# The last pair of row tiles of a feed-forward stage taken token third by token third, and a wait of its own for each table of the rotation

## The reference

```python
def _layer_norm(x, g, b):
    xc = xf - jnp.mean(xf, -1, keepdims=True)
    var = jnp.mean(xc * xc, -1, keepdims=True)
    return xc * lax.rsqrt(var + LN_EPS) * g + b

def _post_block(x, mix, w1, w3, w2, g1, b1, g2, b2):
    x = _layer_norm(ALPHA * x + mix, g1, b1)
    ff = (jax.nn.silu(x @ w1) * (x @ w3)) @ w2
    return _layer_norm(ALPHA * x + ff, g2, b2)
```

## Time and profile before

| | |
|---|---|
| median of 3 runs | 3449.32 us (3448.13 to 3454.1) |
| the profiled execution's own time | 3458.74 us |
| its span | 3457.0 us, 48614 instructions |
| mean granted TensorE clock | 0.913 of full speed |
| PE busy | 3005.5 us, 87%, 19603 matmuls |
| DVE, ACT, POOL busy | 1620.0 us (47%), 835.4 us (24%), 245.8 us (7%) |
| matmul of 128 x 352, float32 (L163 to L165) | 322 to 329 ns each, overlapping |
| add from PSUM to `k.xT` (L848), 24 a pair | 521 ns each |
| cast of a pair of weight tiles, 128 x 2048 (L155) | 1220 ns each |
| TensorE clock in 40 slices of the span, tenths | 9999899986899999999997995558999999999998 |
| PE busy in the same slices, tenths | 8998799969899999999995978007889999999995 |

### The profile page before, as it was taken

The page is one execution under the profiler, slowest core; times in us unless marked ns, Lnnn a source line. Parts: engine busy times, 40 slices in busy tenths (PEclk is TensorE's granted clock), DMA queues, the critical chain, the costliest instruction groups (busy, mean ns, idle before and its releaser), DMA issues. The chain is left out here.

```text
span 3457.0 us, 48614 instructions
## 1 busy us (share of the span) xinstructions
PE 3005.5 (87%) x19603; PEld 2730.4 (79%) x19603; DVE 1620.0 (47%) x3000; ACT 835.4 (24%) x1555; POOL 245.8 (7%) x279
## 2 busy tenths in 40 slices
PE   8998799969899999999995978007889999999995
PEld 8998466538799999999995956004589999999995
DVE  2111288747464443334445134996356333443336
ACT  2110166632432000000013112645433000000002
POOL 2000100005000000000001820002200000000000
PEclk9999899986799999999997995558999999999998
DMA  6222310040211011111101430001020111011101
GB/s 232 98 86 106 116 50 2 1 150 33 89 37 62 37 47 40 57 42 38 40 11 59 127 120 1 1 0 50 1 74 37 49 62 38 37 49 38 62 13 50
DMA packets 63287, 193.63 MB, mean 56 GB/s; under 512 B 7812, under 2 KB 32292, under 8 KB 53792
## 3 DMA queue, kind: packets, MB, share of 16 engines
q1 hardware_dynamic: 58176, 172.86, 14.2%
q0 software_dynamic: 3904, 12.46, 1.2%
q10 hardware_dynamic: 1008, 5.41, 0.4%
HBM read 159.68 MB, written 35.36 MB: 56 GB/s over the span
## 5 line engine op out<-in xcount | busy, mean ns | idle before, releaser
L163 PE MATMUL f_up<-f_x_high,f_w_first 128*128 128x352 f32 x1056 | 347.8, 329 | 21.8 <-issue 21.8
L165 PE MATMUL f_up<-f_x_high,f_w_first 128*128 128x352 f32 x1056 | 345.2, 327 | 0.0
L163 PE MATMUL f_up<-f_x_high,f_w_second 128*128 128x352 f32 x1056 | 344.6, 326 | 0.0
L164 PE MATMUL f_up<-f_x_low,f_w_first 128*128 128x352 f32 x1056 | 342.8, 325 | 0.0
L165 PE MATMUL f_up<-f_x_high,f_w_second 128*128 128x352 f32 x1056 | 342.6, 324 | 0.0
L164 PE MATMUL f_up<-f_x_low,f_w_second 128*128 128x352 f32 x1056 | 340.3, 322 | 0.0
L834 DVE TENSOR_TENSOR f_gated<-f_silu,f_up 128x352 f32<-128x352 f32 x120 | 62.5, 521 | 571.6 <-PE f_up L165 571.6
L163 PE MATMUL f_down<-f_h_high,f_w_high 128*128 128x352 f32 x960 | 314.3, 327 | 14.6 <-DVE xT_sb L871 5.7
L164 PE MATMUL f_down<-f_h_low,f_w_high 128*128 128x352 f32 x960 | 309.6, 323 | 0.0
L165 PE MATMUL f_down<-f_h_high,f_w_low 128*128 128x352 f32 x960 | 309.4, 322 | 0.0
L848 DVE TENSOR_TENSOR xT_sb<-xT_sb,f_down 128x352 f32<-128x352 f32 x384 | 198.6, 521 | 160.6 <-PE f_down L165 160.6
(11 more groups left out here) (467 smaller groups left out, 5891.5 us busy)
## 6 DMA issues: line engine op xcount, KB each, us to landing
f_raw<-w SPq DMA_DIRECT2D x66, 1024.0 KB, 4.8
pe<-pe_y SPq DMA_DIRECT2D x27, 528.0 KB, 2.9
pe_raw<-w_in_e SPq DMA_DIRECT2D x27, 512.0 KB, 4.0
po<-po_y SPq DMA_DIRECT2D x14, 528.0 KB, 2.9
po_raw<-w_in_o SPq DMA_DIRECT2D x14, 512.0 KB, 4.2
xT_sb<-xT ACTq DMA_DIRECT2D x4, 1056.0 KB, 11.5
ro_x<-po SPq DMA_DIRECT2D x8, 528.0 KB, 4.5
y<-xT_sb SPq DMA_DIRECT2D x3, 1408.0 KB, 5.2
```

Source lines behind the costliest of these rows:

```text
L163: pe.matmul(out, wh, xh, start=n == 0, stop=False)
L164: pe.matmul(out, wh, xl, start=False, stop=False)
L165: return pe.matmul(out, wl, xh, start=False, stop=n == depth - 1)
```

## The change

In `rope`, each table gets a semaphore of its own, and each engine waits only for the table that it reads. The order of the loads becomes rotm, first row tile, sin, cos. In the last pair of `project_and_feed`, PE now makes both tiles for one third, and then multiplies this third by w2 for all 8 output tiles, before it goes to the next third; silu and the hidden state follow in that order on ACT and DVE. The layer norm of a finished third goes among the up matmuls of the next, and its reciprocal and scaling among that third's adds. The w2 parts of the last pair go to `late_high` and `late_low`, which share the places of `raw13` and `raw2`. The squares of the second layer norm go to `oT`, and their sums to the place of `x_high` (`over_high`).

```diff
@@ rope
-        consts, scaled, swapped, turned, done, stored = map(st.sem, ("consts", "scaled", ...))
+        scaled, swapped, turned, done, stored = map(st.sem, ("scaled", ...))
+        rot_loaded, cos_loaded, sin_loaded = map(st.sem, ("rot_loaded", "cos_loaded", "sin_loaded"))
+                sp.dma_start(rotm[:], k.d["c_rot"]).then_inc(rot_loaded, 16)
                 load(0)
-                for dst, src in ((rotm, "c_rot"), (cos, "c_cos"), (sin, "c_sin")):
-                    sp.dma_start(dst[:], k.d[src]).then_inc(consts, 16)
+                sp.dma_start(sin[:], k.d["c_sin"]).then_inc(sin_loaded, 16)
+                sp.dma_start(cos[:], k.d["c_cos"]).then_inc(cos_loaded, 16)
...
-                pool.wait_ge(consts, 48)
+                pool.wait_ge(cos_loaded, 16)
...
-                pe.wait_ge(consts, 48)
+                pe.wait_ge(rot_loaded, 16)
...
-                dve.wait_ge(consts, 48)
+                dve.wait_ge(sin_loaded, 16)
@@ project_and_feed, buffers
+        with Stage(nc, name + "_aside0") as tmp:
+            over_high = tmp.sb("s", [P, KT, T])
         high = st.sb("x_high", [P, KT, T], F32R)
-        raw13 = st.sb("raw13", [P, 2, KT, P])
+        with Stage(nc, name + "_raw") as tmp:
+            raw13 = tmp.sb("13", [P, 2, KT, P])
+        late_high = st.sb("late_high", [P, 2, KT, P], F32R)
...
-        raw2 = st.sb("raw2", [P, 2, KT, P])
+        with Stage(nc, name + "_raw_") as tmp:
+            raw2 = tmp.sb("2", [P, 2, KT, P])
+        late_low = st.sb("late_low", [P, 2, KT, P], F32R)
...
+            bank = {0: 0, 1: 1, NCH: 1, NCH + 1: 0, NCH + 2: 1}
@@ project_and_feed, PE
-                make(2 * LAST, 0)
-                make(2 * LAST + 1, 1)
...
-                    return first13[:, 0, f - 2, m], first13[:, 1, f - 2, m]
+                    return late_high[:, f - 2, m], late_low[:, f - 2, m]
...
-                pe.wait_ge(w2_split, LAST + 1)
-                pe.wait_ge(h_split, PAIRS * 2 * NCH)
                 for c in range(NCH):
+                    for f in range(2):
+                        s = 2 * NCH * LAST + 2 * c + f
+                        if c == 0:
+                            pe.wait_ge(w13_split, 2 * LAST + f + 1)
+                        pe.wait_ge(h_split, s - NCH + 1)
+                        if c == 2 and f == 0:
+                            pe.wait_ge(root, NCH + 1)
+                        half(f, c, s % NCH, 0, gate)
+                        if c and f == 0:
+                            mean(NCH + c - 1)
+                        half(f, c, s % NCH, 1, value)
+                    if c:
+                        variance(NCH + c - 1)
+                    pe.wait_ge(w2_split, PAIRS)
+                    pe.wait_ge(h_split, 2 * NCH * LAST + 2 * c + 2)
                     for m in range(KT):
                         n = c * KT + m
                         pe.wait_ge(added, (LAST - 1) * outs + n - 1)
                         multiply(pe, down[:, n % 2, 0:CH], lambda f: weights(f, m), lambda f: hidden(f, c), 4).then_inc(product, 1)
-                        if c and m == 2:
-                            mean(NCH + c - 1)
-                    if c:
-                        variance(NCH + c - 1)
@@ project_and_feed, ACT
-                step(act, LAST, 0)
                 for c in range(NCH):
-                    square(NCH + c)
-                    deviation(NCH + c)
-                    affine(NCH + c)
+                    for f in range(2):
+                        s = 2 * NCH * LAST + 2 * c + f
+                        silu(s, s % NCH)
+                        if c and f == 0:
+                            square(NCH + c - 1)
+                        if c == 0 and f == 0:
+                            act.wait_ge(product, (LAST - 1) * outs)
+                        hidden_high(s, f, c)
+                    if c:
+                        deviation(NCH + c - 1)
+                        affine(NCH + c - 1)
+                square(2 * NCH - 1)
+                deviation(2 * NCH - 1)
+                affine(2 * NCH - 1)
@@ project_and_feed, DVE
-                steady(LAST, 0, 0)
-                dve.wait_ge(w2_loaded, PAIRS * 16)
-                dve.wait_ge(value, (2 * LAST + 1) * NCH)
-                split_on(dve, w2_high, PAIRS, w2_split, raw2[:], first13[:, 0], first13[:, 1])
-                steady(LAST, 0, 1)
...
+                for c in range(NCH):
                     j = NCH + c - 1
+                    for f in range(2):
+                        s = 2 * NCH * LAST + 2 * c + f
+                        if c and f == 0:
+                            centre(j)
+                        hidden(s, 0, f, c, s % NCH)
+                        if c and f == 0:
+                            sum_squares(j)
+                        if c == 0 and f == 0:
+                            dve.wait_ge(w2_loaded, PAIRS * 16)
+                            split_on(dve, w2_high, PAIRS, w2_split, raw2[:], late_high[:], late_low[:])
+                    if c:
+                        invert(j)
+                        add_last(c, [0, 1])
+                        scale(j)
+                        add_last(c, range(2, KT))
                     else:
+                        add_last(c, range(KT))
                     sum_up(j + 1)
-                invert(2 * NCH - 2)
-                scale(2 * NCH - 2)
                 centre(2 * NCH - 1)
                 sum_squares(2 * NCH - 1)
```

More of the change, by code:

```diff
@@ L346, in rope @@
         swap = st.ps("swap", [P, 2, NCH, 512])
-        consts, scaled, swapped, turned, done, stored = map(st.sem, ("consts", "scaled", "swapped", "turned", "done", "stored"))
+        scaled, swapped, turned, done, stored = map(st.sem, ("scaled", "swapped", "turned", "done", "stored"))
+        rot_loaded, cos_loaded, sin_loaded = map(st.sem, ("rot_loaded", "cos_loaded", "sin_loaded"))
         x_loaded = st.slots("x_loaded", RING)
@@ L446, in project_and_feed, with squares, square_sums @@
         spare = lambda j: aside[1 if j == NCH - 1 else 0]
-        squares = lambda j: spare(j)[:, 0:KT * CH].rearrange("p (n t) -> p n t", n=KT)
-        square_sums = lambda j: spare(j)[:, 3 * n_w:3 * n_w + CH]
+        def squares(j):
+            return spare(j)[:, 0:KT * CH].rearrange("p (n t) -> p n t", n=KT) if j < NCH else oT[:, :, cols(j - NCH)]
+        def square_sums(j):
+            return spare(j)[:, 3 * n_w:3 * n_w + CH] if j < NCH else over_high[:, 0, cols(j - NCH)]
         X_high = lambda n, c: high[:, n, cols(c)]
@@ L454, in stats @@
         def stats(j):
-            return (down[:, 0, 0:CH], down[:, 1, 0:CH]) if j == NCH - 1 else (up[:, 0, j % NCH, 0:CH], up[:, 1, j % NCH, 0:CH])
+            bank = {0: 0, 1: 1, NCH: 1, NCH + 1: 0, NCH + 2: 1}
+            return (down[:, 0, 0:CH], down[:, 1, 0:CH]) if j == NCH - 1 else (up[:, 0, bank[j], 0:CH], up[:, 1, bank[j], 0:CH])
         def middle(eng, step):
@@ L871, in add_last @@
                         dve.tensor_tensor(out=xm, in0=xm, in1=down[:, n % 2, 0:CH], op=ALU.add).then_inc(added, 1)
-                add_last(0, range(KT))
-                sum_up(NCH)
-                for c in range(1, NCH):
+                for c in range(NCH):
                     j = NCH + c - 1
[L877 to L882, removed]
-                    else:
[L884 to L888, removed]
+                    for f in range(2):
[13 more added lines that the diff above has]
+                        add_last(c, range(2, KT))
+                    else:
+                        add_last(c, range(KT))
                     sum_up(j + 1)
-                invert(2 * NCH - 2)
-                scale(2 * NCH - 2)
                 centre(2 * NCH - 1)
```

## The result

The changed kernel takes 3440.85 us (median of 19 runs, 3431.91 to 3457.61), the kernel before 3454.18 us beside it (19 runs, of which the 3449.32 above took the first three). The ratio is 0.9962, 95% interval [0.9953, 0.9971]: faster by 0.38%, 13.1 us (10.0 to 16.2). The forecast was 12.0 us.

What follows compares the result with a forecast made beforehand. PE, busy 87% of the span, was taken as the bound, leaving its idle time and work behind its last matmul. Stages 8.2 plus rotations 3.8 gave 12.0 us, from 3449.32 to 3437.3 us; range 3430 to 3446.

Steps and rivals of the forecast that it cites:

- The end of a stage: From the last down matmul's start to the last scaling: 22.1 us instead of 28.1, 6.0 us less per feed-forward stage.
- Bubbles: Last pair: PE waits for the hidden state three times, not once, +4.0 us; variance matmul inside the wait, −0.6.
- The first bubble's second condition: Last pair, first third: w2 must be split before the second hidden tile's gating; +0.3 us per stage.
- Stalls by DVE: Last pair: PE waits less for DVE's centring and scaling, 1.0 us against 2.8, so −1.8 us per stage.
- The clock: Last pair: PE's clock halves after the first bubble only, as before, costing 1.5 us; no fall in the other two.
- Rival 1: Last pairs: the clock falls in the two new bubbles as well, 6.0 us back, 3443.3 us; 13%.
- Table loads: Feed-forward stages: alternating silu and root tables add two loads per stage, 1.28 us each, root 0.02 behind, no drain.
- Rival 3: Each table switch idles a further 1.28 us ahead of the root, 5.1 us back, 3442.4 us; 5%.
- The rotations: Separate table waits: first add 2.85 us earlier, less 0.9 at the end; 1.9 us gained per rotation, 3.8 for two.
- Rival 2: The rotations gain nothing, because POOL and cos set their pace; 3441.1 us; 10%.
- rival 4: Last pairs: w2 lands 7.8 us after issue instead of 4.9, 5.8 us back over both stages, 3443.1 us; 5%.
- rival 5: Last pairs: the low clock outlasts the 12 matmuls after each bubble, kernel slower than before, 3460 us; 7%.

Runs made afterwards that it cites:

- e3: Changed kernel, but DVE makes the middle third's reciprocal and scaling after the last third's adds and sum, as before the change; ratio 0.9986 to the kernel before.
- e5: Changed kernel, but DVE waits for and splits w2 after the first third's second hidden tile instead of before it; ratio 0.9984 to the kernel before.
- e9: The changed kernel itself, run and profiled again; 3443.54 us, ratio 0.9956 to the kernel before.
- e6: Changed kernel, but the rotations load in the old order: first row, rotm, cos, sin; ratio 0.9951 to the kernel before.
- e7: Changed kernel, but the rotations load cos before sin: rotm, first row, cos, sin; ratio 0.9939 to the kernel before.
- e1: Kernel before with only the rotations changed (new `rope`, old `project_and_feed`); ratio 0.9986 to the kernel before, 4.8 us faster.
- e2: Kernel before with only the last pair of each feed-forward stage changed (old `rope`); ratio 0.9977 to the kernel before, 8.0 us faster.
- e4: Changed kernel, but each third first issues 12 down matmuls of the pair before last, then waits for the last pair's operands; ratio 0.9945 to the kernel before.
- e8: As e4, but in the second and third thirds DVE makes two adds before the reciprocal and two more before scaling; ratio 0.9925 to the kernel before.
- e10: The kernel of e8 with cos loaded before sin as in e7; 3430.82 us, ratio 0.9921 to the kernel before.

## Why the prediction was right, step by step

- **The end of a stage** (22.1 forecast instead of 28.1). It measured 22.2 and 22.2. e3 takes away alone what DVE's order gives of it. This step carries the gain of the feed-forward part; the other terms together cost a little. The sign given for it was misread from its own sum: 11.3 is where the squares end. They start at 8.8, by the sum and in the trace.
- **Bubbles** (+4.0, −0.6). Both new gaps are 2.15 from start to start, the variance inside them. Right.
- **The first bubble's second condition** (+0.3). It came to +0.06. The split ended 16.1 us after the pair's start, as I had it, but the gating could not have begun before 15.9 (0.43 behind the last up matmul's start), and it began at 16.0. That the cover is gone is right. e5 shows it, and so does the load's own scatter: where w2 landed after 4.77 us (f0 of e9) the gap was 2.14, where it landed after 5.06 (f0 of e6) it was 2.43.
- **Stalls by DVE** (−1.8, leaving 1.0). Too cautious: there remain 0.1 and 0.15 per third, 0.5 in the stage, −2.3. PE's span up to the last down matmul grew by 1.1 us in f1 (101.97 to 103.07), not 1.9; the two mis-sized terms make the difference.
- **The clock.** One fall per stage, behind the first gap, as before, was forecast. It came in f1, not in f0, and f0 is 1.7 shorter for it. Over all profiles with a first gap of 2.1 to 2.4 the fall came 14 times of 16. The two gaps without it were 2.16 and 2.17, and a gap of 2.14 had one, so their length doesn't tell them apart; what does is open. Behind the gaps with the variance inside it came in none of 28. Rival 1 is refuted.
- **Table loads.** The root starts 0.02 behind the load's end, also here. The drain that the Trainium skill ("ScalarE: Activation LUTs", section What ACT_TABLE_LOAD costs) adds is not in this trace. Rival 3 is refuted.
- **The rotations** (1.9 each). They gained 2.3 and 2.9 us, 1.4 more than forecast for the two. The step that was off is "cos is now the last table, so POOL's start stays": POOL, which waits for the last table, started 7.2 and 6.9 after the first issue, against 8.0 and 8.3. With the small rotm in front, the last of the four loads was there about 1 us sooner. The rest of the term was a little too large. DVE's last add ended 3.57 after POOL's last tile instead of 6.04, 2.47 less, while POOL's row of tiles took 1.0 longer: 1.5 with POOL's start unmoved, not 1.9. DVE's first add started 2.6 after POOL, not 2.4, because its own product ended only then. I had also taken the order for neutral, and it was not: e6 and e7 show that cos should not come last. Rival 2 is refuted by the marks of e1.
- **w2 late** (rival 4): it landed 4.8 after its issue. **Slower** (rival 5): no fall outlasted its 3.4 us except behind e5's gap of 5.55.

The sum, 8.2 + 3.8 = 12.0, stands against 8.0 + 4.8 from e2 and e1, and 13.1 for the whole. By the marks, with a clock fall counted in both stages as forecast, it is 9.6 + 5.2 = 14.8. So the mechanism was right and both parts were under-sized by 1.4 us. That 12.0 lies so near the median's 13.1 is partly luck: the interval, 10.0 to 16.2, holds both.

## What to carry to other kernels

When two loops end in a serial chain, ask what of the chain belongs to work already finished, and put that among matmuls that are still to come; the order in the queue of the engine that runs the chain decided it here (e3), not the busy share. When PE must wait for its newest operand, start accumulation groups with the operands that are old: two groups in two banks hid 1.8 us of a wait of 2 in the first third of each last pair (e4), and in the other thirds the next bound was one engine's order again (e8). Give each consumer its own semaphore, and load first what the engine reads whose work sets the end (here POOL's cos: 1.2 and 1.0 us a rotation in e7).

## What the runs showed that I had not expected

- A load of 64 KB in front of three of 528 KB lands in 1.7 to 1.9 us, behind one of them in 3.5 us, and the whole group is then there about 1 us sooner in the changed kernel than before. Over all profiles the last of the four was there 6.7 to 7.5 us after the first issue with the small load in front, and 7.2 to 8.2 with the row in front, so the two overlap.
- Behind a gap of 2.1 to 2.4 us between matmul starts the granted clock fell 14 times of 16. When it did not, the stage was 1.7 us shorter (f0 of the changed kernel and of e3). With the gap filled it fell in none of six last pairs (e4, e8, e10).
- Two profiles of one kernel differ by 18 us in span (3446.1 and 3428.3), while the last pair of f1, with a clock fall in each, takes 125.2 in both. Of the 18, 8.1 lie ahead of the first rotation (its first load at 333.96 and 325.86), and 5.2 in the first feed-forward stage ahead of its last pair, where the clock fell four times in one profile and once in the other. Why the start differs is open. For a change of 0.4% marks in the trace say more than totals.
